# Summing the rows of the last three expert blocks in PSUM, at the end of each layer of a two-layer diffusion trunk

## The reference, cut to what matters

```python
h = x * (1.0 + sc1) + sh1
y = mixer(h @ w_in[l], ...) @ w_out[l]
x = layer_norm(ALPHA * x + g1 * y, ln1_g[l], ln1_b[l])
def expert_block(tok, e):
    gu = xm[tok] @ w_gu[e]
    return (silu(gu[:, :256]) * gu[:, 256:]) @ w_down[e]
routed = zeros_like(x).at[tok].add(expert_block(tok, e) * weight[:, None])
x = layer_norm(ALPHA * x + g2 * (routed + shared), ln2_g[l], ln2_b[l])
```

## Time and profile before

| | |
|---|---|
| median of 3 runs | 1921.86 us (1921.61 to 1923.24) |
| the profiled execution | 1911.23 us, span 1909.5 us |
| PE matmul busy | 1694.6 us, 89% of the span |
| DVE busy | 854.7 us, 45% |
| ACT busy | 389.9 us, 20% |
| POOL busy | 158.5 us, 8% |
| DMA | 538.98 MB, mean 282 GB/s |

### The profile page before, as it was taken

One profiled execution on the slowest core, in us unless ns is written; L12 is line 12 of the kernel. 1 busy time (PEld: TensorE's weight loads), 2 busy tenths in 40 slices (PEclk: granted clock), 3 DMA queues, 4 the chain that ended last, 5 costly groups with the idle time before them and its releaser, 6 DMA issues. The chain is left out here.

```text
span 1909.5 us, 22774 instructions
## 1 busy us (share of the span) xinstructions
PE 1694.6 (89%) x8463; PEld 917.5 (48%) x8463; DVE 854.7 (45%) x1696; ACT 389.9 (20%) x754; POOL 158.5 (8%) x148
## 2 busy tenths in 40 slices
PE   4999989997999799979779999899979979999783
PEld 1885644643444343434348756455434434444341
DVE  2435425654344343433863444356433434444266
ACT  1323531211111111111122334211111111111111
POOL 0000000230000000000020000015100000000002
PEclk7999989799999899999889999988989999999896
DMA  9534527469989999999234452544798999999950
GB/s 350 170 137 159 198 94 296 183 252 398 397 354 397 411 400 412 397 425 409 84 117 126 143 212 74 226 165 150 296 424 344 394 409 396 420 408 399 423 209 34
DMA packets 103471, 538.98 MB, mean 282 GB/s; under 512 B 36830, under 2 KB 39662, under 8 KB 64060
## 3 DMA queue, kind: packets, MB, share of 16 engines
q1 hardware_dynamic: 91996, 515.24, 68.1%
q0 software_dynamic: 11296, 22.14, 3.1%
q10 hardware_dynamic: 64, 0.07, 0.0%
HBM read 545.95 MB, written 6.59 MB: 289 GB/s over the span
## 5 line engine op out<-in xcount | busy, mean ns | idle before, releaser
L1106 PE MATMUL bank<-ring,arena_a 128*32 128x512 f32 (+2 forms) x2432 | 474.0, 627 | 80.8 <-DMA ring<-in_w_expert_gu 79.9
L1106 PEld LDWEIGHTS bank<-ring,arena_a 128*32 128x32 f32 (+2 forms) x2432 | 164.8, 134 | 357.4 <-issue 356.6
L1682 DVE TENSOR_TENSOR arena_a<-arena_a,bank 128x512 f32<-128x512 f32 x336 | 230.4, 686 | 9.7
L1133 PE MATMUL bank<-arena_b,arena_a 128*32 128x512 f32 (+2 forms) x800 | 212.9, 615 | 18.2 <-DVE arena_a L1671 12.2
L1700 DVE SCALAR_TENSOR_TENSOR arena_a<-arena_a,slot_w,bank 128x256 f32<-128x256 f32 x64 | 30.8, 481 | 442.7 <-ACT arena_a L1968 339.5
L1156 PE MATMUL bank<-ys_hi,to_token 128*128 128x512 f32 x384 | 171.4, 446 | 15.4 <-issue 7.8
L1157 PE MATMUL bank<-ys_lo,to_token 128*128 128x512 f32 x384 | 153.3, 399 | 0.0
L1716 DVE TENSOR_TENSOR ys_lo<-bank,ys_hi 128x512 fp32r<-128x512 f32 x128 | 82.5, 686 | 156.6 <-ACT ys_hi L1976 156.6
L2043 POOL DMA_INDIRECT arena_a<-scratch_x,slot_idx x60 | 61.2, 1019 | 915.9 <-PE bank L1093 859.6
L1968 ACT ACTIVATE arena_a<-bank 128x256 f32<-128x256 f32 x64 | 24.7, 386 | 525.0 <-PE bank L1106 525.0
L1976 ACT ACTIVATE ys_hi<-bank 128x512 fp32r<-128x512 f32 x128 | 69.5, 594 | 273.7 <-PE bank L1133 273.7
(11 more groups left out here) (291 smaller groups left out, 2003.2 us busy)
## 6 DMA issues: line engine op xcount, KB each, us to landing
ring<-in_w_expert_gu SPq DMA_DIRECT2D x128, 2048.0 KB, 13.2
arena_b<-in_w_expert_down SPq DMA_DIRECT2D x88, 1024.0 KB, 17.4
ring<-in_w_mod SPq DMA_DIRECT2D x24, 2048.0 KB, 7.8
arena_a<-in_w_expert_down SPq DMA_DIRECT2D x40, 1024.0 KB, 18.1
ring<-in_w_in SPq DMA_DIRECT2D x10, 2048.0 KB, 12.8
ring<-in_w_out SPq DMA_DIRECT2D x4, 2048.0 KB, 7.8
arena_b<-mods SPq DMA_DIRECT2D x8, 512.0 KB, 9.8
arena_a<-mods SPq DMA_DIRECT2D x8, 512.0 KB, 10.0
```

Of the source, the lines that this page charges most:

```text
L1106: ins = pe.matmul(psum[0][r:r + w, :], xT[:, k, r:r + w], ring_view(gu_slot(n))[:, k, :], start=(k == 0), stop=(k == KD - 1))
L1133: ins = pe.matmul(psum[5 + f][r:r + w, :], hT[b % 2][:, k, r:r + w], down[n % ND][:, k, CH * f:CH * f + CH], start=(k == 0), stop=(k == 1))
L1682: ins = dve.tensor_tensor(z, z, bank[:, :], ALU.add)
```

## The change

The rows of the last three blocks (29 to 31, `KEPT` is 29) are no longer added by DVE one unit at a time. PE sums them in PSUM: six banks (`SUM_BANK`), one for each unit, are opened by block 29, continued by block 30 and closed by block 31 (`sum_rows`). DVE multiplies each finished bank with the gate and adds it once, in the norm (`from_units`). Blocks 30 and 31 get buffers of their own for the split rows and the zero-one matrices, over buffers that are free by then.

The gate and the residual (`gate_sum`) are made a tile at a time in the iteration of block 30: tile 0 ahead of block 29's split, tiles 1 and 2 behind block 30's hidden rows, all ahead of block 31's gate-up result. PE's order at the end becomes: gate-up of 31, the first two units of block 29, the turning of 31's hidden rows, the branch, down projection of 30, the other four units of 29, down projection of 31, sums of 30, sums of 31. In the old order the sums of 29, the down projection of 30, the turning and the sums of 30 stood ahead of the branch.

The low part of the next layer's first weights moves from DVE's end of the first layer to DVE's start of the second; ACT's high part moves behind the split of block 31. The residual of tile 1 moves from POOL to DVE. The overflow branch gets buffers and banks that the new order leaves free; that part, which is jumped over, is left out of the diff here.

```diff
 UNIT_BANK = [1, 4, 5, 6, 1, 4]
-GATED_FROM = NB - 3
+SUM_BANK = [1, 7, 2, 3, 0, 4]
+KEPT = NB - 3
...
+        xg_at = TILES * DM
+        to_token_of = [to_token] * (NB - 2) + [rounded(f"to_token{i}", "arena_a", TOK, xg_at + TOK * i) for i in range(2)]
+        hi_of = [ys_hi] * (NB - 2) + [rounded("hi_m", "arena_b", DM, 0), rounded("hi_n", "arena_a", DM, xg_at + DM)]
+        lo_of = [ys_lo] * (NB - 2) + [rounded("lo_m", "arena_b", DM, DM), ys_lo]
...
                     if b > 1:
-                        pe.wait_ge(added, UNITS * (b - 1))
+                        pe.wait_ge(added, UNITS * min(b - 1, KEPT))
...
-                        pe.wait_ge(added, UNITS * (b - 1) + 4)
+                        pe.wait_ge(added, min(UNITS * (b - 1) + 4, UNITS * KEPT))
...
+                def sum_rows(b, units):
+                    first, last = b == KEPT, b == NB - 1
+                    for u in units:
+                        t, f = u // 2, u % 2
+                        bank = psum[SUM_BANK[u]]
+                        if u == 0:
+                            pe.wait_ge(to_token_ready, b + 1)
+                            pe.wait_ge(ys_ready, 2 * (b + 1))
+                        if first:
+                            if u == 0:
+                                pe.wait_ge(added, UNITS * KEPT)
+                            elif u == 1:
+                                pe.wait_ge(sy_ready, 2 * TILES)
+                            elif u < 4:
+                                pe.wait_ge(xT_ready, NB)
+                            elif u == 4:
+                                pe.wait_ge(hid_ready, NB)
+                            else:
+                                pe.wait_ge(hT_ready, NB)
+                        cols = slice(CH * f, CH * f + CH)
+                        rows_of = to_token_of[b][:, P * t:P * t + P]
+                        pe.matmul(bank[:, :], rows_of, hi_of[b][:, cols], start=first, stop=False)
+                        ins = pe.matmul(bank[:, :], rows_of, lo_of[b][:, cols], start=False, stop=last)
+                        if last:
+                            ins.then_inc(added_full, 1)
...
-                for b in range(NB):
+                for b in range(NB - 1):
...
-                add_rows(NB - 2, range(UNITS))
+                gate_up(NB - 1)
+                sum_rows(KEPT, range(2))
+                turn_hidden(NB - 1)
                 pe.wait_ge(most_ready, 1)
                 with pe.If(pe.value_load(most[0:1, 0:1], min_val=0, max_val=TOK + P) > P):
...
+                down_rows(NB - 2)
+                sum_rows(KEPT, range(2, UNITS))
                 down_rows(NB - 1)
-                add_rows(NB - 1, range(UNITS))
+                sum_rows(NB - 2, range(UNITS))
+                sum_rows(NB - 1, range(UNITS))
                 if has_next:
                     for _ in range(18):
-                        pe.matmul(psum[7][:, :], ident, cst[:, 0:CH], start=True, stop=True)
+                        pe.matmul(psum[5][:, :], ident, cst[:, 0:CH], start=True, stop=True)
...
-                if l == 0:
+                if l:
+                    low_win(0, 0)
+                    low_win(0, 1)
+                else:
...
-                    elif b < GATED_FROM:
+                    else:
                         ins = dve.tensor_tensor(z, z, bank[:, :], ALU.add)
-                    else:
-                        ins = gated_add(t, f, bank)
...
-                def gate_sum():
-                    dve.wait_ge(norm_loaded, 128)
-                    for t in range(TILES):
-                        link(dve.tensor_tensor(acc[:, t, :], acc[:, t, :], gateb[:, 0 if t == 0 else 1, :], ALU.mult))
-                        link(dve.scalar_tensor_tensor(out=acc[:, t, :], in0=x[:, t, :], scalar=ALPHA, in1=acc[:, t, :], op0=ALU.mult, op1=ALU.add))
+                def gate_sum(t):
+                    link(dve.tensor_tensor(acc[:, t, :], acc[:, t, :], gateb[:, 0 if t == 0 else 1, :], ALU.mult))
+                    link(dve.scalar_tensor_tensor(out=acc[:, t, :], in0=x[:, t, :], scalar=ALPHA, in1=acc[:, t, :], op0=ALU.mult, op1=ALU.add))
...
-                for b in range(NB):
+                        dve.tensor_tensor(lo_of[b][:, cols], psum[5 + f][:, :], hi_of[b][:, cols].bitcast(F32), ALU.subtract).then_inc(ys_ready, 1)
+                for b in range(NB - 1):
                     hidden(b)
                     if b > 1:
                         for u in range(UNITS):
                             add_unit(b - 2, u)
                     if b:
                         token_rows(b - 1)
+                        if b == KEPT + 1:
+                            dve.wait_ge(norm_loaded, 128)
+                            gate_sum(0)
                         rows_out(b - 1)
                     hidden_turned(b)
+                    if b == KEPT + 1:
+                        gate_sum(1)
+                        gate_sum(2)
...
-                    if b == GATED_FROM + 1:
-                        gate_sum()
-                for u in range(UNITS):
-                    add_unit(NB - 2, u)
-                if has_next:
-                    for j in range(2):
-                        ks = slice(4 * j, 4 * j + 4)
-                        dve.wait_ge(next_hi, j + 1)
-                        dve.tensor_tensor(w_lo[0][:, ks, :], ring_view(0)[:, ks, :], win_hi[:, ks, :].bitcast(F32), ALU.subtract).then_inc(next_lo, 1)
+                hidden(NB - 1)
+                hidden_turned(NB - 1)
...
-                token_rows(NB - 1)
-                rows_out(NB - 1)
+                for b in (NB - 2, NB - 1):
+                    token_rows(b)
+                    rows_out(b)
                 def from_units(t, z, g, which):
                     for f in range(2):
-                        add_unit(NB - 1, 2 * t + f)
+                        u, cols = 2 * t + f, slice(CH * f, CH * f + CH)
+                        dve.wait_ge(added_full, UNITS * KEPT + u + 1)
+                        link(dve.tensor_tensor(gated_part, psum[SUM_BANK[u]][:, :], g[:, cols], ALU.mult))
+                        link(dve.tensor_tensor(z[:, cols], z[:, cols], gated_part, ALU.add))
                     if t:
                         scale_shift(which, t - 1)
                 norm(1, from_units)
-                dve.wait_ge(normal_ready, 2 * TILES)
-                residual(TILES - 1)
-                dve.wait_ge(residual_ready, TILES + 1)
-                if has_next:
-                    dve.wait_ge(next_lo, 2)
+                for t in range(1, TILES):
+                    dve.wait_ge(normal_ready, TILES + t + 1)
+                    residual(t)
+                dve.wait_ge(residual_ready, 2 * TILES - 1)
...
-                        act.wait_ge(added_full, UNITS * b)
+                        act.wait_ge(added_full, UNITS * min(b, KEPT))
...
-                    if b:
+                    if 0 < b < NB - 1:
                         rows_high(b - 1)
...
-                rows_high(NB - 1)
+                for b in (NB - 2, NB - 1):
+                    rows_high(b)
+                if has_next:
+                    act.wait_ge(preloaded[0], 16)
+                    act.wait_ge(y_full, BLOCK_OF[E - NG - 1] + 1)
+                    for j in range(2):
+                        ks = slice(4 * j, 4 * j + 4)
+                        act.activation(win_hi[:, ks, :], ring_view(0)[:, ks, :], ACT.Copy).then_inc(next_hi, 1)
                 norm(1)
+                if has_next:
+                    act.wait_ge(next_hi, 2)
...
-                for t in range(TILES - 1):
-                    pool.wait_ge(normal_ready, TILES + t + 1)
-                    pool.tensor_tensor(xm[:, t, :], xm[:, t, :], lnb[:, 0, :], ALU.mult).then_inc(pool_scaled, 1)
-                    pool.wait_ge(pool_scaled, t + 1)
-                    pool.tensor_tensor(x[:, t, :], xm[:, t, :], lnb[:, 1, :], ALU.add).then_inc(pool_residual, 1)
-                pool.wait_ge(pool_residual, TILES - 1)
+                pool.wait_ge(normal_ready, TILES + 1)
+                pool.tensor_tensor(xm[:, 0, :], xm[:, 0, :], lnb[:, 0, :], ALU.mult).then_inc(pool_scaled, 1)
+                pool.wait_ge(pool_scaled, 1)
+                pool.tensor_tensor(x[:, 0, :], xm[:, 0, :], lnb[:, 1, :], ALU.add).then_inc(pool_residual, 1)
+                pool.wait_ge(pool_residual, 1)
```

More of the change, by code:

```diff
@@ L73 @@
 UNIT_BANK = [1, 4, 5, 6, 1, 4]
-OVER_BANK = [0, 1, 2, 3, 4, 7]
-GATED_FROM = NB - 3
+SUM_BANK = [1, 7, 2, 3, 0, 4]
+OVER_BANK = [0, 2, 3, 4, 5, 6]
+KEPT = NB - 3
 MODC = 6 * DM // CH
@@ L751, in _ @@
                     for t in range(TILES):
-                        if t < TILES - 1:
-                            sp.wait_ge(pool_residual, t + 1)
+                        if t == 0:
+                            sp.wait_ge(pool_residual, 1)
                         else:
-                            sp.wait_ge(residual_ready, TILES + 1)
+                            sp.wait_ge(residual_ready, TILES + t)
```

(18 more changed lines are left out.)

22 lines of the change are left out of this document (11 added, 11 removed).

## The result

The changed kernel takes 1874.59 us (median of 4 runs, 1871.45 to 1883.23) against 1921.73 (4 runs, 1918.31 to 1923.24) for the kernel before: a ratio of 0.9764, 95% interval 0.9729 to 0.98, some 38 to 52 us less. That is faster, as forecast, but by more than the predicted 28 us, and outside the range of 1886 to 1906. The profiled execution took 1875.72, with a span of 1873.7.

A forecast was written before the change was run, and what follows sets the result against it. The chain hopping between PE and DVE in each layer's tail was taken as the bound; first layer 17.3, second 14.2, second layer's start -3.4, together 28.1 us off, gave 1894 us, range 1886 to 1906 (8 in 10).

The forecast's parts named there:

- Branch: 4.8, to 922.0: First layer's tail, ahead of block 30's down projection: PE's overflow branch, register load to next matmul, keeps 4.8 us.
- I take 6.1: Block 30's down projection after some 4.3 us of PE idling: 6.1 us; bounds 3.65 (full clock) and 7.3 (half).
- the branch is short: Rival: PE's overflow branch takes DVE's 0.07 us, PE holds its clock; gain 40 in all, 1882; chance 0.06.
- the tails: Last gate-up to norm in each layer: 13.1 us less in the first, 13.0 in the second.
- The norm's tail: Norm's end in each layer: DVE takes tile 1's residual from POOL and ends 0.8 us sooner.
- the barrier: First layer's end: POOL's drain no longer last; gain 4.2 us with DVE's 0.8 included, bounds 3.3 and 4.2.
- the second layer's end: End of the second layer, where POOL's drain and SyncE's end close together: 0.8 and 0.4 us more gained.
- the low weights: Second layer's start: 4.49 us of DVE work comes first, PE's input projection waits; cost 3.4 us.
- POOL's drain is tied to POOL's own work: First layer's end: assumed by the forecast; the rival, drain tied to the other engines' end, gives 1898, chance 0.07.
- the clock in the second layer's projection comes back: Second layer's input projection: assumed after about 4 us idle; the rival, half clock throughout, costs 99 us, 1993; chance 0.04.

The follow-up runs named there:

- after_shift64: Changed kernel with 64 further instructions, waits already met, at the start of PE's program: 1894.67 us, ratio 0.9895.
- after_shift68: Changed kernel with 68 instead of 64 further instructions at the start of PE's program: 1892.65 us, ratio 0.9862.
- after_shift64_near: Changed kernel with 64 further PE instructions at the start and two rounds instead of three in PE's overflow body (jump of 198): 1875.15 us, ratio 0.9794.
- after_shift128: Changed kernel with 128 further instructions at the start of PE's program: 1874.08 us, ratio 0.975.
- gate_late: Changed kernel with gate and residual of all three tiles made behind block 30's hidden rows, as before: 1887.59 us, ratio 0.9828.
- residual_on_pool: Changed kernel with tile 1's residual back on POOL, its store waiting for POOL again: 1887.36 us, ratio 0.9828.
- low_in_gaps_dve: Changed kernel with next layer's low weights in DVE's tail waits, high weights ahead of ScalarE's branch, and all residuals on DVE: 1874.26 us, ratio 0.9741.

## Why the prediction was off

**The step that failed** is "Branch: 4.8, to 922.0", and with it "I take 6.1" for the down projection of block 30 (the 6.09 us at 941.22, behind 4.08 us of idle time and at a granted clock of 0.50; after_shift64, with the long branch, has 5.71 and 6.22). From the register's load to the next matmul are 1.6 us (922.2 to 923.78), not 4.8, and the projection takes 3.67. I had this as the rival "the branch is short" with a chance of 0.06, at 1882, because 3.66 and 3.73 agreed in both layers. But both layers' branches stand at the same place within each 256 instructions (174 and 173), and in every run of the table both are long or both short: one observation, not two. The change took some instructions from ahead of the branch (61 in the first layer, 8878 to 8817 by the count), and that decided it: 64 put back made it long again (after_shift64). The rows ahead of the prediction show no transfer of code; the DMA view of the branch's window does: one packet of 16 KB in each of the two branches.

**What held.** With the branch long the tails are 13.5 and 13.2 us shorter (after_shift64) where 13.1 and 13.0 were forecast. The norm's tail gained 1.0 (0.8 forecast), the barrier 3.3 more (with the 0.8, 4.4 against 4.2), the second layer's end 1.8 against 1.2, the low weights cost 3.3 against 3.4. Together 29.5 us by stages with a long branch (28.1 forecast), 40.4 with a short one (40). The mechanisms were right, also that POOL's drain is tied to POOL's own work, and that the clock in the second layer's projection comes back: granted 0.50 until 975, 0.93 in the 2 us behind it.

**The range** was too narrow at its lower end: a branch whose length I could not explain was given its old length with 0.94, when its bounds (0.07 us on DVE, 3.7 on PE) were known, and these turned out to be 11 us apart over both layers.

**What stays open.** The medians differ by more than the stages. From before to after they are 47 us apart, and the stages give 40.4. (The two profiled executions are only 35.8 us of span apart, mostly because the first layer's last gate-up ended at 921.19 in that of after and at 916.17 in that of before: 5.0 us later, by a stretch that the change doesn't touch.) By stages the long branch costs 10.9 us, but after_shift64 and after_shift68 lie 19.5 and 18.6 us above the kernels with a short one that were measured on the same chip (after_shift64_near and after_shift128). So by medians the branch is worth the whole 19 us between 1894 and 1874.59, by stages 11 of them. after_shift64, which has the tail that was forecast, lies 22 us below before, where its stages give 29.5. gate_late and residual_on_pool cost 6.5 and 6.1 by stages and 13 by medians (against after_shift128, same chip). In after_shift64 the profiled execution was the shortest of six (1885.0 at a mean granted clock of 0.939); the longest took 1901.7 at 0.929. Time by clock is the same in both, 1770 and 1767, so the longer ones fit a lower clock, but where in the run it was lower, no trace recorded. The clock does differ between profiles in stretches that no edit touches, as in these windows of the second layer, 140 us after its start, of after and of after_shift128:

```profile
1101.03:1121.03 20.00, 19.70 (x128) 11.71 (x129) 8.47 (x32) 9.31 (x38) 0.00 (x0) 0.99 0.54 209
```

```profile
1097.19:1117.19 20.00, 19.79 (x105) 10.31 (x98) 5.35 (x21) 5.69 (x21) 0.00 (x0) 0.74 0.32 114
```

Whether a delay in a tail makes such falls likelier was not settled.

## What to carry to other kernels

A duration that no work explains is not a property of the instruction: ask what it waits for (here the DMA view of its window) before it is carried to another place. Keep the body that a branch jumps over short: here jumps of 100 and 198 instructions were short at a place where 296 was long, and the cost of the long jump depended on instructions added or taken away ahead of it (64 at the program's start took the branch from 0.38 to 3.69 us). And a gap on PE can cost itself plus the half clock behind it: in gate_late a 1.8 us delay cost 4.65 in one layer, where the granted clock fell to 0.50, and 1.85 in the other, where it stayed at 1.00.

## What the runs showed of the hardware

A taken branch on PE takes 0.24 to 0.45 us, or 3.4 to 3.7 with a code packet of 16 KB in it; on DVE 0.07. DVE's fp32 addition of two SBUF operands (128 x 512) takes 0.69 us, and 2.00 while POOL multiplies and adds in SBUF (after, 946.71 and 949.47, beside POOL's 945.82 to 950.93); the product with a PSUM operand stays at 0.69 beside it (948.74). With POOL doing nothing there all twelve additions take 0.69 (low_in_gaps_dve).
